# Two-layer hybrid block: tokens in groups of 256, with the next group's merge, output projection and norm issued beside the current group's gathers

## What is computed

```python
def _merge(oa, ob, oc, gates, wa, wb, wc, wo):
    ga, gb, gc = jnp.split(jax.nn.sigmoid(gates), 3, axis=-1)
    y = ga * (oa @ wa) + gb * (ob @ wb) + gc * (oc @ wc)
    return y @ wo
def _peer(h, w_q, subkeys, u_tab, v_tab):
    q = (h @ w_q).reshape(t, PEER_HEADS, 2, PEER_QDIM // 2)
    s = jnp.einsum('thid,hind->thin', q, subkeys)
    s_top, i_top = lax.top_k(s, PEER_TOPK)
    ...
    best, pos = lax.top_k(cand, PEER_TOPK)        # 8 heads x 16 picks = 128 experts a token
    act = gelu(einsum('td,thkd->thk', hb, u_tab[ib]))
    return einsum('thk,thkd->td', gb * act, v_tab[ib])
# in a layer: x = x + mx[2] * merge(...);  h = modulate(rmsnorm(x));  x = x + mx[5] * peer(h)
```

## Time and profile before

| | us |
|---|---|
| median of 3 runs | 6765.36 (6759.11 to 6768.72) |
| the profiled execution: its time | 6770.41 |
| its span, first to last instruction | 6768.6 |
| TensorE busy | 5562.9 (82%) |
| VectorE busy | 3232.7 (48%) |
| ScalarE busy | 1679.4 (25%) |
| GpSimd busy | 1287.7 (19%) |
| TensorE in `accumulate`, L1522 | 2422.9 |
| TensorE in the merge, L1185 (gates) and L1190 (three branches) | 427.6 and 3 x 71.4 |
| TensorE in the projections of L387 with `yT` (`w_out`) | 144.2 |
| mean granted TensorE clock | 0.949 |

### The profile page before, as it was taken

One profiled execution on the slowest core, in us unless ns is written; L12 is line 12 of the kernel. 1 busy time (PEld: TensorE's weight loads), 2 busy tenths in 40 slices (PEclk: granted clock), 3 DMA queues, 4 the chain that ended last, 5 costly groups with the idle time before them and its releaser, 6 DMA issues. The chain is left out here.

```text
span 6768.6 us, 54389 instructions
## 1 busy us (share of the span) xinstructions
PE 5562.9 (82%) x18084; PEld 2922.8 (43%) x18084; DVE 3232.7 (48%) x7126; ACT 1679.4 (25%) x4406; POOL 1287.7 (19%) x1284
## 2 busy tenths in 40 slices
PE   6989987999888777777777787999799788777777
PEld 2488644555444333333332234985344333333322
DVE  1357205201366766676764324660231266766654
ACT  1410124200222332223232223100430133332322
POOL 0000000000133333333333200000000133433333
PEclk8989998999899999999999998989799899999999
DMA  6000010211488999999999840001022398999998
GB/s 194 28 1 0 31 45 4 56 42 39 168 304 302 422 421 414 419 415 415 419 417 420 335 140 12 1 0 52 28 56 56 122 353 336 421 421 421 421 420 355
DMA packets 372133, 1510.07 MB, mean 223 GB/s; under 512 B 61266, under 2 KB 173012, under 8 KB 207572
## 3 DMA queue, kind: packets, MB, share of 16 engines
q0 software_dynamic: 184320, 1342.26, 48.7%
q1 hardware_dynamic: 152020, 160.19, 7.4%
q10 hardware_dynamic: 35584, 5.12, 0.5%
HBM read 1505.38 MB, written 2.10 MB: 223 GB/s over the span
## 5 line engine op out<-in xcount | busy, mean ns | idle before, releaser
L1522 PE MATMUL ps<-ring,diag 128*128 128x512 f32 x5120 | 2422.9, 614 | 742.9 <-ACT diag L1439 733.5
L1398 POOL DMA_INDIRECT ring<-peer_uv,picks x1280 | 1287.5, 1006 | 5442.8 <-DVE picks L1625 3335.8
L1642 DVE CUSTOM_DVE_ANT_0 ring<-ring,hn 128x1024 f32<-128x1024 f32 x1280 | 1561.2, 1223 | 1002.2 <-DMA ring<-peer_uv,picks 998.4
L1522 PEld LDWEIGHTS ps<-ring,diag 128*128 128x128 f32 x5120 | 944.1, 193 | 2128.1 <-ACT diag L1439 1134.5
L1428 ACT ACTIVATE acts<-dots 128x2 f32<-128x2 f32 x640 | 130.1, 203 | 2052.5 <-DVE dots L1642 2052.3
L1439 ACT ACTIVATE diag<-consts,wgt 128x128 f32<-128x128 f32 x1280 | 445.0, 394 | 23.9 <-PE ps L1522 2.9
L1185 PE MATMUL ps<-hT,wg 128*128 128x512 f32 (+1 forms) x1152 | 427.6, 528 | 17.9 <-DMA wb<-w_branch_c 11.0
L1502 PE MATMUL ps<-hT,wq 128*128 128x512 f32 (+1 forms) x768 | 317.5, 536 | 8.5 <-DMA wq<-peer_wq 8.5
L1432 ACT ACTIVATE wgt<-gates,acts 128x1 f32<-128x1 f32 x1280 | 308.0, 287 | 61.1 <-ACT acts L1428 2.2
L1185 PEld LDWEIGHTS ps<-hT,wg 128*128 128x128 f32 x1152 | 220.0, 192 | 220.2 <-issue 209.9
L801 PE MATMUL ps<-hT,w 128*128 128x512 f32 (+1 forms) x832 | 297.5, 518 | 20.0 <-DMA w<-w_in 16.1
(11 more groups left out here) (267 smaller groups left out, 5639.5 us busy)
## 6 DMA issues: line engine op xcount, KB each, us to landing
w<-w_mod SPq DMA_DIRECT2D x24, 2048.0 KB, 7.9
w<-w_in SPq DMA_DIRECT2D x28, 1024.0 KB, 5.3
wg<-w_in SPq DMA_DIRECT2D x48, 512.0 KB, 6.0
ring<-peer_uv,picks POOLq DMA_INDIRECT x1280
wq<-peer_wq SPq DMA_DIRECT2D x32, 512.0 KB, 6.0
w<-w_in SPq DMA_DIRECT2D x4, 2048.0 KB
w<-w_out SPq DMA_DIRECT2D x8, 1024.0 KB, 6.0
mixing<-mixing_dram ACTq DMA_DIRECT2D x2, 2432.0 KB, 9.5
```

Source lines behind the costliest of these rows:

```text
L1398: pool.indirect_dma_start(out=ring[:, n % S, :], out_offset=None, in_=table, in_offset=bass.IndirectOffsetOnAxis(ap=picks[:, half(i), p:p ...
L1522: last = pe.matmul(ps[:, total_bank(i), 512 * b:512 * (b + 1)], diag[:, n % DIAGS], ring[:, n % S, D + 512 * b:D + 512 * (b + 1)], start=( ...
L1642: dve.tensor_tensor_reduce(out=row, in0=row, in1=hn[:, half(i)], scale=1.0, scalar=0.0, op0=ALU.mult, op1=ALU.add, accum_out=dots[:, half( ...
```

## The change

The tokens are cut into groups of 256 (two tiles): 3 groups in layer 0, 2 in layer 1. `merge`, `add_mixed` and `norm` become one function `mix_group` for one group. The first group's runs by itself ahead of `experts` (`mix_alone`, a stage with 24 merge units, 8 output units and the norm). The later groups' are written into `experts`: `mix_group` gives each engine's program as a generator that stops ahead of each unit, and `Beside.advance(slot)` runs it on as far as a plan says, at the end of each pick (slot) of the group before. The plan: 18 units over the 128 picks of the first tile, the other 26 over the first 54 picks of the second tile. A merge unit is 12 products of 256 columns on TensorE, one sigmoid on ScalarE, one to two operations on VectorE. Queries are computed per group, 6 of the 16 blocks in the last 64 picks of the group before and 10 in the first 80 picks of its own. The ring has 6 slots in both layers. Weights for the merge, for `w_out` and for the queries are loaded once per group instead of once per layer, one unit per DMA (768 KB and 512 KB) in contiguous pieces. `accumulate` uses one PSUM buffer for the sum instead of two in turn and runs two picks at a time, behind every odd pick.

```diff
-RING = (7, 9)
+GROUP = 2 * P
+RING = 6
...
+class Beside:
+    def advance(self, slot):
+        for j, (plan, program) in enumerate(self.plans):
+            due = plan(slot)
+            if due and self.begun[j] is None:
+                self.begun[j] = 0
+                self.begun[j] = next(program, 1 << 30)
+            while due and self.begun[j] < due:
+                self.begun[j] = next(program, 1 << 30)
...
+    def mix_group(self, s, l, at, branches, yT, sq, earlier=None):
+        MERGES = 3 * KD
+        FIRST, OUT, NORM = 3, 3 + MERGES, 3 + MERGES + KD + 1
...
+        def sync_program(sp):
...
+            for n in range(2, MERGES + KD):
+                yield FIRST + n - 1
+                sp.wait_ge(multiplied, n - 1)
+                load(n)
+        def tensor_program(pe):
...
+            for m in range(MERGES):
+                yield FIRST + m
+                pe.wait_ge(loaded[m % 2], 16 * (m // 2 + 1))
...
+                for k in range(KD):
+                    pe.matmul(bank(m)[:, 0:G], w[:, m % 2, k], self.hT[:, k, tok], start=(k == 0), stop=(k == KD - 1))
+                for k in range(HB):
+                    last = pe.matmul(bank(m)[:, G:2 * G], w[:, m % 2, KD + k], branches[m % 3][:, k, tok], start=(k == 0), stop=(k == HB - 1))
+                last.then_inc(multiplied, 1)
+            for b in range(KD):
+                yield OUT + b
...
+                if b:
+                    pe.wait_ge(added, b)
+                for k in range(KD):
+                    last = pe.matmul(bank(0)[:, 0:G], w[:, n % 2, k], yT(k), start=(k == 0), stop=(k == KD - 1))
+                last.then_inc(multiplied, 1)
+                if b:
+                    sum_squares(b - 1)
+        def scalar_program(act):
...
+            for m in range(MERGES):
+                yield FIRST + m
+                act.wait_ge(multiplied, m + 1)
+                if m >= 2:
+                    act.wait_ge(taken, m - 1)
+                act.activation(sg[:, m % 2], bank(m)[:, 0:G], ACT.Sigmoid).then_inc(opened, 1)
+        def vector_program(dve):
...
+            for m in range(MERGES):
+                yield FIRST + m
+                dve.wait_ge(opened, m + 1)
...
+                to = acc[:, 0] if m % 3 == 0 else part[:, m % 2]
+                dve.tensor_tensor(to, sg[:, m % 2], bank(m)[:, G:2 * G], ALU.mult).then_inc(taken, 1)
+                if m % 3:
+                    dve.wait_ge(taken, m + 1)
...
+            def plan(g):
+
+                units, a = mixes[g - 1].units, (g - 1) * SLOTS
+                early, last = 18, SLOTS - 74
+
+                def due(slot):
+                    n = slot - a
+                    if n < 0:
+                        return 0
+                    if n < PICKS:
+                        return (n + 1) * early // PICKS
+                    return min(units, early + (n - PICKS + 1) * (units - early) // (last - PICKS) + 1)
+                return due
...
+            def query_step(slot):
+
+                g, n = slot // SLOTS, slot % SLOTS
+                if n < KD * (NB - 6):
+                    return g, 6 + n // KD, n % KD
+                n -= SLOTS - 64
+                if 0 <= n < 6 * KD and g + 1 < NG:
+                    return g + 1, n // KD, n % KD
+                return None
...
                 @block.tensor
+                        if r < R - 1 and p == 100:
+                            turn_h(r + 1)
+                        if r and p == 4:
+                            turn_sum(r - 1)
+                        for n in (p - 1, p) if p % 2 else ():
+                            accumulate(r, n)
+                        if step := query_step(slot):
+                            query(*step)
+                        side.advance(slot)
...
                 @block.scalar
+                        if p % 2:
+                            weights(r, p - 1)
+                        side.advance(slot)
...
                 @block.vector
+                        dot(r, p)
+                        side_stages.advance(slot)
```

More of the change, by code:

```diff
@@ L1304, in experts @@
+        self.rotate(l, lam_init, qT, kT, lam)
+        self.attend(qT, kT, vda, lam, ycT, lo)
+        self.free = merged
+        self.mix_alone(l, lo, (oaT, ybT, ycT))
+        self.experts(l, lo, (oaT, ybT, ycT))
+        self.free = begin
+    def experts(self, l, lo, branches):
         nc, ps = self.nc, self.ps
         first, end = lo // P, TILES
+        R = end - first
+        NG = R // 2
         NEG = -3.0e38
         NB = 2 * PH
-        S = RING[l]
+        S = RING
         DIAGS = 4
-        LEAD = 14
+        SLOTS = 2 * PICKS
@@ L1311, in experts @@
         before = list(self.gathered_counts)
-        for n in range((end - first) * PICKS):
+        for n in range(R * PICKS):
             self.gathered_counts[n % S] += 16
@@ L1372, in half @@
-            def half(i):
-                return (i - first) % 2
-            def tile_choice(p, shift):
-                q = p - 4 + shift
-                return q // LEAD if 0 <= q and q % LEAD == 0 and q // LEAD < PH else None
+            yaT, ybT, ycT = branches
+            mixes, plans = [], []
+            at = self.free
+            for g in range(1, NG):
+                self.free = at
+                mixes.append(self.mix_group(s, l, lo + g * GROUP, branches,
+                                            lambda k: (yaT if k < HEADS else ybT)[:, k % HEADS, 0:GROUP], ycT[:, :, 0:GROUP],
+                                            mixes[-1].ready if mixes else None))
@@ new lines, in plan @@
+            def plan(g):
[9 more added lines that the diff above has]
+                return due
+            plans = [plan(g) for g in range(1, NG)]
@@ new lines, in beside, with choice @@
+            def beside(programs):
+                return Beside(programs, plans)
+            def choice(r, kb):
+                g, second = r // 2, r % 2
+                if not second:
+                    return NB * g + (0 if kb == 0 else 2 * kb - 1)
+                return NB * g + (2 * kb + 2 if kb < PH - 1 else NB - 1)
+            def query_step(slot):
[6 more added lines that the diff above has]
+                return None
@@ L1566, in _ @@
-                    turn_sum(end - 1)
+                    turn_h(0)
+                    for b in range(2):
+                        for k in range(KD):
+                            query(0, b, k)
+                    scores(0, 0)
+                    for b in range(2, 6):
+                        for k in range(KD):
+                            query(0, b, k)
+                    for slot in range(R * PICKS):
+                        r, p = slot // PICKS, slot % PICKS
+                        g, second = r // 2, r % 2
+                        kb, q = p // TOPK, p % TOPK
+                        if not second:
+                            if q == 0 and kb + 1 < PH:
+                                scores(r, kb + 1)
+                            if q == (6 if kb + 1 < PH else 0):
+                                scores(r + 1, kb)
+                        elif g + 1 < NG and p == PICKS - 40:
+                            scores(r + 1, 0)
+                        if r < R - 1 and p == 100:
[6 more added lines that the diff above has]
+                            query(*step)
+                        side.advance(slot)
@@ L1568, in _, with choose @@
+                    turn_sum(R - 1)
                 @block.vector
                 def _(dve):
+                    side_stages = beside([m.vector(dve) for m in mixes])
                     step = Steps(dve, chosen)
-                    def choose(i, kb, part):
-                        c = choice(i, kb)
+                    def choose(r, kb, part):
+                        c, half = choice(r, kb), r % 2
                         scores = sc[:, c % 2]
@@ L1723, in hybrid_kernel @@
             k.mixers(l, lo)
-            k.norm(k.gain2, 3, lo)
-            k.experts(l, lo)
         k.store()
```

655 lines of the change are left out of this document (337 added, 318 removed).

## The result

The changed kernel takes 7109.57 us (median of 4 runs, 7105.19 to 7110.72), the kernel before 6766.97 beside it; the ratio is 1.0507, 95% interval [1.0489, 1.0526]. The forecast was 7020, the range 6870 to 7170. The direction and the mechanism were right, the size was 90 us short, and not all terms behind it were right.

What follows compares the result with a forecast made beforehand. Later tiles were taken as DMA-bound, merge and projection as TensorE-bound, mixed groups as held by ties. 2 x 200 + 2 x 36 + 3 x 937 + 2 x 676 = 4635 against 4383, +252 on 6765.4: 7020 us, range 6870 to 7170.

Steps and rivals of the forecast that it cites:

- Wait at a unit, 3.74 us at an even pick: Mixed groups: TensorE waits through sigmoid, VectorE, dot and diagonal after each merge unit, 3.74 us, or 4.97 at odd picks.
- Merge unit and pair at full clock (cycle 12.5): Second tile of a mixed group: merge unit with its wait 9.06 us, plus 3.44 for the pair of picks.
- the choices: First tile of a mixed group: VectorE's choices, 8.5 us each, cost 69 us in full, taken as 43.
- Mixed group 937: 256 picks with the next group's units beside them: 495 us first tile, about 442 second, 937 in all.
- Ring of 6 at nothing: DMA-bound picks: six slots leave 8.4 us for a gather that takes 6.3 unloaded, so no cost.
- rival C: The ring of 6 is short: DMA-bound picks take 2.7 instead of 2.51 us, +118, 7140 us; chance 10%.
- Last group 676: Each layer's last group, without merge beside it: 233 us for 80 picks, the rest near the DMA pace, 676.
- `mix_alone` 200: The first group's merge, projection and norm ahead of the experts: 200 us a layer, bounds 172 and 225.
- Score ties 1.57: First tile: TensorE stands 1.57 us where ScalarE waits for scores before making the next diagonals; 15 such scores.
- Tables at nothing: Merge units: ScalarE's sigmoid and gelu table loads run beside TensorE's unit and the dot, so cost nothing; 1.28 each if uncovered.
- Rival A: Mixed groups: ties hidden, work fits beside the gathers, about 735 us a group, 6415 in all; chance 13%.
- Rival B: Mixed groups: merge weights land late behind the gathers, some 5 us more per closely spaced unit, 7155; chance 7%.

Runs made afterwards that it cites:

- serial_ring7: The changed kernel with all groups merged ahead of the experts, nothing beside the gathers, and a ring of 7 instead of 6: 6668.56 us.
- serial_groups: The changed kernel with every group's merge, projection and norm run ahead of the experts, nothing beside the gathers, ring still 6: 6783.06 us.
- ring7: The changed kernel with a ring of 7 slots in place of 6, nothing else: 6992.14 us.
- fill: The changed kernel with 7 more unused products of 256 columns on TensorE behind each merge unit beside the gathers: 7048.09 us.
- lag_dve: The changed kernel with only VectorE's part of merge units three picks later, ScalarE's sigmoid left in place, ring of 6: 6930.24 us.
- before_scores: The kernel before with ScalarE's copy of the scores moved behind the next pair's weights in each layer's first tile: 6705.09 us.
- lag_scores: The changed kernel with merge units three picks and output units one pick later on ScalarE and VectorE, ring of 7, scores copied two picks later: 6496.78 us.

## Why the prediction was right, and where its sum was not

The difference of 343 us splits over kernels that were run: groups with a ring of 7 and no overlap, -97 (serial_ring7); the seventh slot taken away, +114 (serial_groups against it); the overlap with its ties, +326 (changed against serial_groups). Together +343.

Against the prediction's own terms, on TensorE in us, the three mixed groups in order:

| part | forecast | changed | ring7 | fill |
|---|---|---|---|---|
| first tile | 495 | 510, 510, 507 | 499, 493, 498 | 500, 505, 505 |
| first 36 picks of the second | 203 | 219, 223, 219 | 222, 222, 222 | 204, 205, 204 |
| its last 92 | 237 | 249, 242, 247 | 241, 237, 238 | 244, 244, 245 |
| last group of a layer | 676 | 692, 684 | 659, 658 | 701, 684 |

- *Wait at a unit, 3.74 us at an even pick:* 3.77, 3.31, 3.77 and 3.78 in the dense part; lag_dve's 3.00 confirms the links one by one. Right. The cycle of an output unit, 10.1: right. In the first tile the 15 waits behind a unit are 3.4 to 7.4 us, 74 together against the 66 of the forecast.
- *Merge unit and pair at full clock (cycle 12.5):* mis-sized, 14.3 to 15.2. This is the step that failed in the mixed groups: rows of before showed it already, the four instructions behind the 4.52 us in the earlier trace rows take 2.94 against 1.88, and I read only the wait from them. In the dense part it is the whole error: with the waits filled the 36 picks take the 203 of the forecast. In the first tile all 15 pairs behind a unit are slow as well. That it comes out only 15 us over says that something else in my sum, the choices perhaps, stood too high there.
- *Mixed group 937:* 978, 975 and 974, +116 in all. Of the 39 a group, 18 go with a seventh slot and 24 with fill; no run has both.
- *Ring of 6 at nothing:* wrong. It costs 117 us here, 99 in the kernel before. I compared the 8.4 us that are left for a gather with the 6.3 of a gather with none beside it; with 6 slots the loaded gathers take a median of 8.4, all that there is, and with 7 slots 10.1. (Layer 1 loses three slots by the change, not the two of rival C.) Rival C, given 10%, was true at the size that it named (118), beside the forecast and not in its place.
- *Last group 676:* 692 and 684, +24, by two errors. 33 and 26 of it are the ring; at 7 slots it is 659, so choices and ties beside DMA-bound picks were priced 17 too high. The window shows why: DMA share 0.99 already in its first tile.
- *`mix_alone` 200:* 176, near its lower bound. TensorE is busy 160 of 176 us; the weights come in time. -48 for two. Heads 40 instead of 36, +8.
- *Score ties 1.57:* about 2.0 (before_scores).
- *Tables at nothing:* right; the mixed groups don't get shorter without them. (The working speaks of 42 units at even picks; 7 and 9 in each of three groups are 48.)
- *Rival A:* fell. Ring of 7 leaves the ties (6992). With order, ring and score copies changed the picture is A's after all: 6497, inside its 6415 to 6740, with 149 to 152 us for the 36 picks (A: 136) and 403 to 407 for a first tile (A: 361). The issue order was most of what stood against it.
- *Rival B:* fell. In the mixed first tiles the 768 KB land in 6.4 to 6.5 us, in the dense part in 4.2, and TensorE hardly waits for them; two loads issued where the gathers fill the engines took 14.3, with nobody waiting for them. In the first tile of lag_scores (DMA share 0.96) they take 8.2 and a gather 9.1. The Trainium skill (DMA: Bandwidth & Descriptors, Queues, rings and completion order) has it that a DMA engine takes turns between its queues. The rows of lag_scores fit that rule.

The stretches of the earlier trace rows end 5 us ahead of the last addition in each layer, so the 4383 of before was 10 too low. With that the terms give 252 - 10 - 48 + 8 + 116 + 24 = 342 us, against 343 measured. A forecast that is 1.3% off had errors of -58 and +148 us in it, and that these have different signs is luck: with the +148 alone the kernel would have taken 7168, at the very end of the range.

## What to carry to other kernels

When work is put beside a pipelined loop, list for each engine what it will wait for and what stands behind that wait. If three engines meet at each unit, the consumers' parts belong later in their lists than the producer's, far enough for what the producer needs next to stand ahead of them: one pick was enough at even picks here and not at odd ones, three did for both. That move is worth 451 us where the overlap without it costs 326. Price a wait on TensorE with the matmuls behind it too, and a buffer ring by what a gather takes under load, not alone.

## What was not expected of the hardware

- TensorE's granted clock goes from the upper to the lower of its two levels (2.4 and 1.2 GHz) behind waits of a few us. In the dense part of the changed kernel a pair takes 3.70 us behind waits of 2.53 and 2.96, 5.25 to 6.72 behind 3.77 and 3.78, 5.40 behind 3.31 and, in lag_dve, behind 3.00. Behind 3.67 it takes 5.40, then 6.32, then 3.70. So no single length decides in these rows. The Trainium skill (TensorE: Matmul & The Clock Gate, Why this matters for your kernels) advises against idle gaps between bursts of matmuls. The traces agree, with 0.88 to 0.90 in the tied tiles and 0.97 to 1.00 in the lagged ones.
- Products that nobody needs, 7 per unit, made the changed kernel 61 us faster: in the dense part the clock is 1.00 with them and 0.88 to 0.89 without.
- In the kernel before, DMA engines with a busy share of 0.99 moved 399 GB/s with a ring of 6, and with a share of 1.00 they moved 415 with a ring of 7.
